# Another order of attention, a head loaded ahead, a head's parts per block, and the final norm inside the experts

## The chip, the cores and the metric

The kernel runs on one core of one Trainium2 chip. The metric is device time in microseconds (us), here of that core. TensorE (PE) does the matrix products, VectorE (DVE), ScalarE (ACT) and GpSimd (POOL) do elementwise work, SyncE (SP) issues most transfers. Each engine runs its instructions in order, and engines wait for one another through semaphores.

## What is computed

An encoder layer runs over two groups of tokens with shared weights: 1024 tokens ("prompt", the short group, g = 0) and 2048 tokens ("sample", the long group, g = 1), with D = 1024. The input is normalised, scaled and shifted by values made from a condition vector, and projected by w_in to latent queries and keys, a rotary key and four pooling groups u. Eight heads of attention (queries and keys 64 + 32 wide, values 64 wide) run within each group; beside them each pooling group takes mean minus value over a window of 2, 4, 8 or 16 tokens. Both go through an output projection to a gated residual. Then each of 16 experts takes its best tokens (128 of the short, 256 of the long group), runs them through a gated feed-forward of width 1024, and adds the weighted result to its tokens' rows. A last RMS normalisation with a gain closes it:

```python
def encoder_layer(x, c, ...):
    h = rmsnorm(x) * (1 + sc1) + sh1
    z = h @ w_in
    att = latent_attention(c_q, c_kv, k_pe, q_norm_g, kv_norm_g, w_uq, w_ukv)
    pool = multiscale_pool(u, w_pool, pool_scale)
    x = x + g1 * (jnp.concatenate([att, pool], axis=-1) @ w_out)
    h = rmsnorm(x) * (1 + sc2) + sh2
    return x + g2 * expert_choice_ffn(h, w_router, w_gate, w_up, w_down)
# trunk: return rmsnorm(encoder_layer(x, c), final_norm_g)
```

## The kernel before

Every product is made in three parts from a rounded high part and the remaining low part of each operand; so most data exists twice, ScalarE writes the high parts and VectorE or GpSimd the low ones. The program is a row of stages that hand results on through device memory (s_ct, s_qn, s_kn, s_v, s_x and so on). A stage ends for all engines at once: nothing of the next starts before its last store has landed. The order within a stage is written out by hand, per engine, and SyncE's queue of transfers is in order too. `build` (L2354) calls the stages.

`in_proj` (L100): w_ada and w_in come through a ring of five raw buffers, with SyncE waiting for the user of a buffer (`load_raw`, L211). The modulation values come from w_ada (`early`, `late`), the input blocks of 256 tokens are squared (`stats`, ScalarE), scaled by GpSimd (L279), transposed by TensorE (`turn`, L483; L493) and modulated by ScalarE (`modulate`, L300). `w_high` (L284, L287) and `w_low` (L401) split the w_in chunks. Then 24 tiles of 128 tokens are projected; per tile SyncE stores u (L253), s_ct and s_kr. After tile 17 SyncE also stores the four gate vectors, 4 bytes an element (L260 to L267), ahead of the load of a later input block (L209).

`latent_proj` (L597): six blocks of 512 tokens, for each 16 entries of ORDER (products for keys, queries, values and the rotary part), each followed by a high copy, a low subtraction and a store. Beside it GpSimd pools u in 12 jobs of 1024 columns (JOBS, L610): fetch by SyncE, 1 to 4 additions, a multiplication, a subtraction, and a store (L782) by SyncE at two points of each block.

`attention` (L935) is called for g = 1, then g = 0. It loads a head's queries, keys and values at its start (`load_qk`, L1037; `load_v`), memsets the rows with constants (L1310), and then takes heads in turn (HU = 2 or 4 heads have buffers), loading the next head in a loop while it works. For each block of 512 queries TensorE first makes a product for the row maxima (`unit`, L1106), then scores, exponentials, and values, and a sum. SyncE stores each block's result (L1047), folds the denominators and stores inverses (L1065). 

`experts` (L1940): for each expert, six chunks of weights (four of gate and up, two of down) are loaded, split by ScalarE (L2167) and VectorE (L2214) and multiplied. The down products (L2142 to L2144) run over 3 slots of 128 tokens for the first output half, then for the second; VectorE weighs each (L2269) into `ye`; after the last weighing GpSimd issues three indirect additions into s_x (L2078). Slot 0 holds the short group's tokens, slots 1 and 2 the long group's.

`final_norm` (L2280) is a stage of its own: 12 blocks of 256 tokens, through four buffers, loaded by SyncE (L2312), squared by ScalarE (L2330, L2333), scaled by VectorE (L2347, L2350) into a second set of buffers, and stored by ScalarE's queue.

## Time and profile before

| | us |
| --- | --- |
| median of 3 runs (lowest, highest) | 3949.04 (3944.26, 3949.94) |
| the profiled execution | 3950.72 |
| its span on the core | 3948.9 |
| TensorE busy in the span | 3577.4 (91%) |
| VectorE, ScalarE, GpSimd busy | 2024.3, 1885.9, 1348.1 |
| mean granted clock of TensorE (of full speed) | 0.941 |

Read it so: one execution was traced; the span runs from its first to its last instruction. Stages are seen by which lines run. In the trace the input projection takes 0 to 448, the latent projection to 656, the long group's attention to 1481, the short group's to 1717, output weights and output projection to 2090, selection to 2190, the experts to 3882, and the final normalisation to the end.

### The profile page before, as it was taken

To read this page: it belongs to the slowest core of one execution; us is meant where nothing else is said; L and a number is where in the kernel's file an instruction comes from. 1 tells how busy PE (TensorE), PEld (TensorE's weight loads), DVE (VectorE), ACT (ScalarE), POOL (GpSimd) and SP (SyncE) were. 2 spreads that over 40 slices of the span, in tenths; PEclk is the share of its full clock that TensorE was granted. 3 is DMA by queue.
4 is the path that set the end of the run, shared out by engine and by line. 5 is a ranking of instruction groups with operands and counts; after the bars stand their busy time and mean duration, and the time that the engine had idled before them with its cause. 6 is when DMAs were issued, how large, how long until landed. Compare 5 with 4: busy or idle time off the path is not lost. (4 is left out here: it accounts for less than half of the span.)

```text
span 3948.9 us, 54396 instructions
## 1 busy us (share of the span) xinstructions
PE 3577.4 (91%) x19090; PEld 3094.5 (78%) x19090; DVE 2024.3 (51%) x3145; ACT 1885.9 (48%) x3250; POOL 1348.1 (34%) x1008
## 2 busy tenths in 40 slices
PE   7999795999999998969993799999999999999991
PEld 5999684777777765747772799999999999999990
DVE  3332353888888876832226644444444444444433
ACT  3433221888888886843330334443443444444433
POOL 1111175988888887842221000000000000000000
PEclk8999897999999998989995899999999999999995
DMA  6444599022122206236541354455444444454437
GB/s 229 160 157 91 195 394 302 18 44 43 43 44 44 43 8 129 49 110 189 176 157 51 128 160 151 147 159 159 147 150 147 142 147 150 156 159 154 144 101 276
DMA packets 363781, 538.93 MB, mean 136 GB/s; under 512 B 38816, under 2 KB 256208, under 8 KB 360656
## 3 DMA queue, kind: packets, MB, share of 16 engines
q1 hardware_dynamic: 339600, 448.60, 36.4%
q0 software_dynamic: 13824, 50.34, 5.2%
q10 hardware_dynamic: 10176, 37.75, 2.4%
q8 instruction: 92, 1.51, 0.2%
q14 instruction: 89, 0.73, 0.1%
HBM read 394.07 MB, written 142.46 MB: 136 GB/s over the span
## 5 line engine op out<-in xcount | busy, mean ns | idle before, releaser
L1314 POOL TENSOR_TENSOR att_pr<-att_e,att_pr 128x512 fp32r<-128x512 f32 x640 | 812.6, 1292 | 152.1 <-ACT att_pr L1201 141.5
L2078 POOL DMA_INDIRECT s_x<-moe_ye,moe_to_add x48 | 90.9, 1893 | 1437.6 <-DVE moe_ye L2269 1427.8
L1245 DVE TENSOR_REDUCE att_mx<-att_m_ps 128x1 f32<-128x512 f32 x640 | 423.5, 682 | 116.0 <-PE att_m_ps L1106 106.2
L2214 DVE TENSOR_TENSOR keep_wl<-keep_raw,keep_wh 128x1024 fp32r<-128x1024 f32 x380 | 440.0, 1220 | 33.6 <-ACT keep_wh L2167 33.6
L2167 ACT ACTIVATE keep_wh<-keep_raw 128x1024 fp32r<-128x1024 f32 x380 | 369.9, 1045 | 126.0 <-PE moe_d_ps L2144 126.0
L1147 PE MATMUL att_o_ps<-att_pr,att_v 128*128 128x512 f32 x1280 | 410.3, 402 | 4.8 <-POOL att_pr L1314 4.6
L1195 ACT ACTIVATE att_e<-att_s_ps 128x512 f32<-128x512 f32 x640 | 378.4, 591 | 69.7 <-PE att_s_ps L1135 24.2
L1201 ACT ACTIVATE att_pr<-att_e 128x512 fp32r<-128x512 f32 x640 | 402.8, 629 | 18.4 <-issue 2.7
L1267 DVE TENSOR_TENSOR att_acc_ps<-att_acc_ps,att_e 128x512 f32<-128x512 f32 x544 | 375.0, 689 | 16.6 <-ACT att_e L1195 11.0
L2194 ACT ACTIVATE moe_silu<-moe_a_ps 128x384 f32<-128x384 f32 x128 | 62.9, 492 | 645.1 <-PE moe_u_ps L2117 645.1
L2115 PE MATMUL moe_a_ps<-moe_xh,keep_wh 128*128 128x384 f32 x1024 | 345.5, 337 | 2.1 <-DVE moe_xl L2222 2.1
L2252 DVE TENSOR_TENSOR moe_hf<-moe_u_ps,moe_silu 128x384 f32<-128x384 f32 x128 | 71.3, 557 | 536.5 <-ACT moe_silu L2194 536.5
L2117 PE MATMUL moe_a_ps<-moe_xh,keep_wl 128*128 128x384 f32 x1024 | 344.7, 337 | 0.0
L2116 PE MATMUL moe_a_ps<-moe_xl,keep_wh 128*128 128x384 f32 x1024 | 344.7, 337 | 0.0
L2117 PE MATMUL moe_u_ps<-moe_xh,keep_wl 128*128 128x384 f32 x1024 | 344.1, 336 | 0.0
L2115 PE MATMUL moe_u_ps<-moe_xh,keep_wh 128*128 128x384 f32 x1024 | 344.1, 336 | 0.0
L2116 PE MATMUL moe_u_ps<-moe_xl,keep_wh 128*128 128x384 f32 x1024 | 344.1, 336 | 0.0
L2142 PE MATMUL moe_d_ps<-keep_wh,moe_hh 128*128 128x512 f32 x768 | 312.0, 406 | 0.0
L2144 PE MATMUL moe_d_ps<-keep_wh,moe_hl 128*128 128x512 f32 x768 | 303.6, 395 | 0.0
L2143 PE MATMUL moe_d_ps<-keep_wl,moe_hh 128*128 128x512 f32 x768 | 302.7, 394 | 0.0
L1147 PEld LDWEIGHTS att_o_ps<-att_pr,att_v 128*128 128x128 f32 x1280 | 243.5, 192 | 67.6 <-POOL att_pr L1314 12.0
L1106 PE MATMUL att_m_ps<-att_k,att_q 96*128 96x512 f32 x640 | 236.8, 412 | 60.6 <-DMA att_k<-s_kr 60.6
(276 smaller groups left out, 7675.3 us busy)
## 6 DMA issues: line engine op xcount, KB each, us to landing
keep_raw<-w_gate SPq DMA_DIRECT2D x64, 1024.0 KB, 5.1
keep_raw<-w_up SPq DMA_DIRECT2D x64, 1024.0 KB, 7.6
keep_raw<-w_down SPq DMA_DIRECT2D x64, 1024.0 KB, 6.6
inp_raw<-w_ada SPq DMA_DIRECT2D x48, 512.0 KB, 5.9
s_ct<-inp_ct SPq DMA_DIRECT2D x24, 640.0 KB, 3.1
prj_ct<-s_ct SPq DMA_DIRECT2D x6, 2560.0 KB, 15.2
s_kn<-prj_out SPq DMA_DIRECT2D x24, 512.0 KB, 11.8
s_qn<-prj_out SPq DMA_DIRECT2D x24, 512.0 KB, 11.9
```

The lines of the kernel that those rows point to most:

```text
L1147: mm = nc.tensor.matmul(o_ps[b % 2][:, :], v[:, h, kt, :], pr[:, s % RING, a, :], start=(kt == 0 and a == 0), stop=(kt == NT - 1 and a == 1))
L1195: nc.scalar.activation(e[:, s % RING, :], s_ps[s % 2][:, :], ACT.Exp, scale=SCALE).then_inc(exp_done, 1)
L1201: nc.scalar.activation(pr[:, s % RING, 0, :], e[:, s % RING, :], ACT.Copy).then_inc(hi_done, 1)
L1245: nc.vector.tensor_reduce(mx[:, u % CB, u // CB:u // CB + 1], m_ps[u % MB][:, :], AX, ALU.max).then_inc(max_part, 1)
L1267: step = nc.vector.tensor_tensor(acc_ps[:, :], acc_ps[:, :], e[:, s % RING, :], ALU.add)
L1314: nc.gpsimd.tensor_tensor(pr[:, s % RING, 1, :], e[:, s % RING, :], pr[:, s % RING, 0, :].bitcast(F32), ALU.subtract).then_inc(lo_done, 1)
L2115: nc.tensor.matmul(out, hi, xh[:, k, :], start=(k == 0), stop=False)
L2116: nc.tensor.matmul(out, hi, xl[:, k, :], start=False, stop=False)
L2117: mm = nc.tensor.matmul(out, lo, xh[:, k, :], start=False, stop=(k == KD - 1))
L2142: nc.tensor.matmul(out, h_hi, wh[:, c % 2, k, :], start=(k == 0), stop=False)
L2167: nc.scalar.activation(wh[:, s, part, :], raw[:, s, part, :], ACT.Copy).then_inc(w_hi_done, 1)
L2214: nc.vector.tensor_tensor(wl[:, s, part, :], raw[:, s, part, :], wh[:, s, part, :].bitcast(F32), ALU.subtract).then_inc(w_lo_done, 1)
```

## The change

- The input projection: ScalarE makes the first three high parts of w_in before the first modulations and one after; VectorE's low parts follow them; in tile 0 the transposes of block 1 come after the u products, and ScalarE's statistics of tile 0 come ahead of the next modulation. The gates are stored by ScalarE's queue after tile 17.
- The latent projection: pooling in 24 jobs of 512 columns, four a block at entries 2, 6, 10 and 14 of ORDER; GpSimd's last addition writes the sum to diff, and VectorE makes the difference from the mean in one operation (`difference`). The first two fetches of u are issued before w_uq. Rows of ones and zeros are stored to s_rows. After block 2's stores SyncE loads the short group's first head (queries, keys, rows: 7 parts) into kept memory.
- Attention: the short group comes first; head 0's values are loaded at its start and heads 1 to 3 by `load_part`, eight parts a head, rows of constants among them (in place of GpSimd's memsets). During its 16 blocks SyncE loads one part a block of the long group's two first heads, and waits for all of them before the last store.
- Experts: the last expert's down products go slot by slot, both halves of one slot after another, and each slot's addition is issued once its two weighings are done. The final normalisation is part of this stage: in place, in four buffers that lie in the raw weights' memory; the first four blocks (the short group's) are loaded after slot 0's addition, the others after those of slots 1 and 2. VectorE takes block j - 2 behind weighing j. The final_norm stage is gone.

The diff, cut to its core:

```diff
-                if n == len(LATE) + 1:
-                    sp.wait_ge(mod_done, len(EARLY) + len(LATE))
-                    for a, part in enumerate((2, 5)):
-                        for g in range(2):
-                            at = (2 * a + g) * D
-                            sp.dma_start(w["s_gates"][0, at:at + D].rearrange("(k p) -> p k", p=P),
-                                         keep["modc"][:, g, part * KD:(part + 1) * KD],
-                                         allow_slow_non_contiguous=True).then_inc(gates_stored, 16)
...
+            def store_gates():
+                act.wait_ge(mod_done, len(EARLY) + len(LATE))
+                for a, part in enumerate((2, 5)):
+                    for g in range(2):
+                        at = (2 * a + g) * D
+                        act.dma_start(w["s_gates"][0, at:at + D].rearrange("(k p) -> p k", p=P),
+                                      keep["modc"][:, g, part * KD:(part + 1) * KD],
+                                      allow_slow_non_contiguous=True).then_inc(gates_stored, 16)
...
             for half in range(2):
-                if half:
-                    for k in range(PAIRS):
-                        w_high(k)
+                for k in range(3 * half, PAIRS if half else 3):
+                    w_high(k)
                 for c in (2 * half, 2 * half + 1):
                     modulate(0, c)
...
+                    n = TB * b + j
+                    if n == 0:
+                        latent_stats(n)
                     if b + 1 < NB:
                         modulate(b + 1, 2 * j)
-                    latent_stats(TB * b + j)
+                    if n:
+                        latent_stats(n)
                     if b + 1 < NB:
                         modulate(b + 1, 2 * j + 1)
                     latent_high(TB * b + j)
+                    if TB * b + j == len(LATE) + 1:
+                        store_gates()
...
+            for k in range(2):
+                w_low(k)
+            copy_rows(2, u_ps[0][:, :])
+            w_low(2)
             for c in range(2):
                 h_low(0, c)
-            for i in range(2):
-                for k in (2 * i, 2 * i + 1):
-                    w_low(k)
-                copy_rows(2 + i, u_ps[i][:, :])
+            w_low(3)
+            copy_rows(3, u_ps[1][:, :])
...
+                    if n == 0:
+                        for c in range(2):
+                            h_low(1, c)
...
-                    if n == 0:
-                        turn(1, 0)
-                    if b + 1 < NB:
+                    if b + 1 < NB and n:
                         turn(b + 1, 2 * j + 1)
...
+                    if n == 0:
+                        for c in range(2):
+                            turn(1, c)
...
+def load_part(sp, w, g, n, heads, i, part, sem):
+
+    S = SEQS[g]
+    NT = S // P
+    tokens = slice(STARTS[g], STARTS[g] + S)
+    q, k, v = heads[i]
+    if part < 4:
+        dst, src = ((q[0:NOPE], w["s_qn"][:, n + i, :, tokens]), (q[NOPE:QK], w["s_qr"][:, n + i, :, tokens]),
+                    (k[0:NOPE], w["s_kn"][:, n + i, :, tokens]), (k[NOPE:QK], w["s_kr"][:, :, tokens]))[part]
+        src = src.rearrange("l r t -> r l t")
+    elif part < 7:
+        dst, row = ((k[QK:QK + 1, 0], 1), (k[QK:QK + 1, 1], 0), (q[QK:QK + 1, 1], 0))[part - 4]
+        src = w["s_rows"][row:row + 1, 0:S]
+    else:
+        dst = v
+        src = w["s_v"][TILE0[g]:TILE0[g] + NT, :, (n + i) * 2 * VD:(n + i + 1) * 2 * VD].rearrange("t p c -> p t c")
+    sp.dma_start(dst.bitcast(F32), src).then_inc(sem, 16)
+
+
 def latent_proj(nc, w, keep):
...
-    SPAN = min(SEQS)
+    SPAN = BANK
...
+    JOBS_PER = len(JOBS) // NB
+    POINTS = [PER * (i + 1) // JOBS_PER - 2 for i in range(JOBS_PER)]
...
+                for lev in range(c + 1):
+                    r = 1 << lev >> 1
+                    lo, hi = 2 * r + (lev == 0), SPAN + 2 * PAD - 2 * r + (lev > 0)
+                    src = sums[:, (lev - 1) % 2] if lev else x
+                    before, behind = (src[:, lo - r:hi - r], src[:, lo + r:hi + r]) if lev else (src[:, lo - 1:hi - 1], src[:, lo:hi])
+                    if lev == c:
+                        cut = slice(PAD - lo, PAD - lo + SPAN)
+                        nc.gpsimd.tensor_tensor(diff[:, n % 2], before[:, cut], behind[:, cut], ALU.add).then_inc(total_ready, 1)
+                    else:
+                        done = step(nc.gpsimd.tensor_tensor(sums[:, lev % 2, lo:hi], before, behind, ALU.add))
+                        pool.wait_ge(summed, done)
...
             load(0)
+            for n in range(2):
+                fetch(n)
             sp.dma_start(qraw[:], w["w_uq"][0].rearrange("(k p) n -> p k n", p=P)).then_inc(q_in, 16)
...
-                    if at in (PER // 3, 2 * PER // 3):
-                        n = 2 * b + int(at > PER // 2)
+                    if at in POINTS:
+                        n = JOBS_PER * b + POINTS.index(at)
...
+                if b == SEQS[0] // BANK:
+                    sp.wait_ge(w_lo_done, ALL_PIECES)
+                    for slot in range(SLOTS):
+                        sp.wait_ge(stored[slot], 16 * b)
+                    for part in range(HEAD_LOADS - 1):
+                        load_part(sp, w, 0, 0, head_tiles(keep, 0, None), 0, part, ahead_in)
...
+            sp.wait_ge(ahead_in, 16 * (HEAD_LOADS - 1))
...
+                c = JOBS[n][1]
+                first, last = ends_of(n)
+                a, b = PAD * first, SPAN - PAD * last
+                dve.wait_ge(total_ready, n + 1)
+                nc.vector.scalar_tensor_tensor(diff[:, n % 2, a:b], diff[:, n % 2, a:b], 1.0 / WINDOWS[c],
+                                               u[:, n % 2, PAD + a:PAD + b], ALU.mult, ALU.subtract).then_inc(diff_ready, 1)
...
+                    if n in POINTS:
+                        difference(JOBS_PER * b + POINTS.index(n))
...
-            load_qk(0, 0)
-            for i in range(HU):
-                sp.dma_start(k[NOPE:QK, i].bitcast(F32), w["s_kr"][:, :, tokens]
-                             .rearrange("l r t -> r l t")).then_inc(kpe_in, 16)
-            load_v(0, 0)
-            for i in range(1, HU):
-                load_qk(i, i)
-                load_v(i, i)
+            if g == 0:
+                load_v(0, 0)
+            for i in range(READY, HU):
+                for part in range(HEAD_LOADS):
+                    load_part(sp, w, g, 0, heads, i, part, rest_in[i])
...
+                    if g == 0:
+                        n = it * NG + b
+                        load_part(sp, w, 1, 0, head_tiles(keep, 1, None), n // HEAD_LOADS, n % HEAD_LOADS, ahead_in)
...
             over_heads(sp, body)
+            if g == 0:
+                sp.wait_ge(ahead_in, 2 * 16 * HEAD_LOADS)
             store(ITERS, -1)
             fold(ITERS, -1)
             store_inverses(ITERS, -1)
...
-            for row, value in ((k[QK:QK + 1, :, 0, :], 1.0), (k[QK:QK + 1, :, 1, :], 0.0), (q[QK:QK + 1, :, 1, :], 0.0)):
-                nc.gpsimd.memset(row.bitcast(F32), value).then_inc(rows_set, 1)
...
+        fin = raw[:].rearrange("p s k n -> p (s k n)").rearrange("p (r j d) -> p r j d", r=R, j=2)
+        gain = rows[:, 0, :]
...
+        def down(last, j):
+
+            return (j // 2, j % 2) if last else (j % SLOTS, j // SLOTS)
...
             over_experts(sp, body)
+            sp.wait_ge(turned, E * KD)
+            sp.dma_start(gain, w["final_norm_g"].partition_broadcast(P)).then_inc(gain_in, 16)
+            sp.wait_ge(w_lo_done, (E * CHUNKS - 1) * PIECES)
+            for b in range(BLOCKS):
+                if b == 0:
+                    sp.wait_ge(added[0], 16 * E)
+                if b == EARLY_BLOCKS:
+                    for s in range(1, SLOTS):
+                        sp.wait_ge(added[s], 16 * E)
+                if b >= R:
+                    sp.wait_ge(y_stored[b % R], 16 * (b // R))
+                src = w["s_x"][b * 2 * P:(b + 1) * 2 * P, :].rearrange("(j p) d -> p j d", p=P)
+                sp.dma_start(fin[:, b % R], src).then_inc(fin_in[b % R], 16)
 
...
-                pool.wait_ge(ye_done, (e + 1) * DOWNS)
+                if not last:
+                    pool.wait_ge(ye_done, (e + 1) * DOWNS)
...
+                    if last:
+                        pool.wait_ge(ye_done, e * DOWNS + 2 * (s + 1))
...
+                for j in range(DOWNS):
+                    s, n = down(last, j)
                     c = GU + n
-                    pe.wait_ge(w_lo_done, (e * CHUNKS + c) * PIECES)
-                    for s in range(SLOTS):
...
+            for b in range(BLOCKS):
+                act.wait_ge(fin_in[b % R], 16 * (b // R + 1))
+                for j in range(2):
+                    if 2 * b + j >= 2:
+                        act.wait_ge(squared, 2 * b + j - 1)
+                    nc.scalar.activation(rows[:, 1 + j, :], fin[:, b % R, j, :], ACT.Square, scale=float(D) ** -0.5,
+                                         accum_out=ms[:, 2 * b + j:2 * b + j + 1]).then_inc(squared, 1)
+                act.wait_ge(squared, 2 * b + 2)
+                nc.scalar.activation(ms[:, 2 * b:2 * b + 2], ms[:, 2 * b:2 * b + 2], ACT.Sqrt,
+                                     bias=eps[:, 0:1]).then_inc(std_done, 1)
+                if b >= 1:
+                    store(b - 1)
+            store(BLOCKS - 1)
...
+                            weigh(e, last, j)
+                if last:
+                    for j in range(DOWNS):
+                        weigh(e, last, j)
+                        if j >= 2:
...
+            def normalise(b):
+
+                if b == 0:
+                    dve.wait_ge(gain_in, 16)
+                dve.wait_ge(std_done, b + 1)
+                nc.vector.reciprocal(ms[:, 2 * b:2 * b + 2], ms[:, 2 * b:2 * b + 2]).then_inc(rstd_done, 1)
+                dve.wait_ge(rstd_done, b + 1)
+                for j in range(2):
+                    nc.vector.scalar_tensor_tensor(fin[:, b % R, j, :], fin[:, b % R, j, :], ms[:, 2 * b + j:2 * b + j + 1],
+                                                   gain, ALU.mult, ALU.mult).then_inc(y_done, 1)
...
-        latent_proj(nc, w, keep)
-        for g in (1, 0):
-            attention(nc, w, keep, g)
+        with ExitStack() as ahead:
+            tile(ahead, "ahead0", [P, 4 * SEQS[0]], F32R, side="right")
+            latent_proj(nc, w, keep)
+            tile(ahead, "ahead1", [P, 2 * (4 * SEQS[1] + SEQS[1] // P * 2 * VD)], F32R, side="right")
+            for g in range(2):
+                attention(nc, w, keep, g)
...
-        moe_ctx.close()
-        final_norm(nc, w, keep)
```

## Rows read from the trace of the kernel before

**Rows 1.** Page, part 2: TensorE busy tenths in 40 slices of 98.7 us
```profile
PE   7999795999999998969993799999999999999991
```

**Rows 2.** Timeline (start us, duration, engine, line, operation, [idle before]) from 0; a window
```profile
21.15 8.83 SPq L232 DMA_DIRECT2D inp_raw<-w_ada  x2
...
26.98 2.25 ACT L287 ACTIVATE inp_wh<-inp_raw 128x1184 fp32r<-128x1184 f32 x2
...
23.33 0.17 DVE L381 TENSOR_TENSOR keep_modc<-inp_c_ps,inp_biasc 128x8 f32<-128x8 f32 x1 [0.65 <-PE inp_c_ps L530]
...
63.93 1.97 PE L493 MATMUL inp_t_ps<-keep_ident,inp_x 128*128 128x128 f32 x8 [5.09 <-POOL inp_x L279]
...
65.00:70.00 5.00, 5.00 (x28) 5.00 (x27) 2.81 (x9) 4.31 (x11) 0.00 (x0) 0.55 0.00 0
```

**Rows 3.** Timeline of SyncE's queue and of ScalarE, 345 to 401 us
```profile
348.08 0.36 SPq L253 DMA_DIRECT2D s_ut<-inp_ut  x1
350.89 2.92 SPq L265 DMA_DIRECT2D s_gates<-keep_modc  x4
353.86 2.05 SPq L209 DMA_DIRECT2D inp_x<-x_sample  x1
362.71 0.36 SPq L253 DMA_DIRECT2D s_ut<-inp_ut  x1
383.66 0.36 SPq L253 DMA_DIRECT2D s_ut<-inp_ut  x1
400.42 0.36 SPq L253 DMA_DIRECT2D s_ut<-inp_ut  x1
...
375.49 1.06 ACT L294 ACTIVATE inp_junk<-inp_x 128x1024 f32<-128x1024 f32 x1 [11.95 <-DMA inp_x<-x_sample]
```

**Rows 4.** Latent projection: a window (DMA share, GB/s last), timelines, a line, a landing
```profile
455.00:640.00 185.00, 168.17 (x720) 137.73 (x720) 98.88 (x136) 56.04 (x100) 125.81 (x95) 0.94 1.02 388
...
645.87 0.34 SPq L782 DMA_DIRECT2D s_diff<-prj_diff  x1
655.99 0.73 SPq L1037 DMA_DIRECT2D att_q<-s_qn  x1
...
677.10 9.52 PE L1106 MATMUL att_m_ps<-att_k,att_q 96*128 96x512 f32 x16 [41.36 <-DMA att_k<-s_kr]
...
L723 POOL TENSOR_TENSOR prj_sums<-prj_u 128x1039 f32<-128x1039 f32 x12 | 23.0, 1917 | 60.4 <-DMA prj_u<-s_ut 60.2 <-POOL prj_diff L751 0.2
...
prj_u<-s_ut SPq DMA_DIRECT2D x8, 516.0 KB, 12.2
```

**Rows 5.** Between the two groups' attentions, the second's end; a landing
```profile
1495.35 4.74 PE L1106 MATMUL att_m_ps<-att_k,att_q 96*128 96x512 f32 x8 [19.27 <-DMA att_k<-s_kr]
...
1481.56 0.64 SPq L1037 DMA_DIRECT2D att_q<-s_qn  x1
...
1709.51 0.34 SPq L1065 DMA_DIRECT2D s_rden<-att_rden  x1
1711.19 0.48 SPq L1047 DMA_DIRECT2D s_att<-att_att  x1
...
att_v<-s_v SPq DMA_DIRECT2D x4, 512.0 KB, 9.7
```

**Rows 6.** The last expert and the final normalisation: timelines, window, landing
```profile
3836.07 0.74 DVE L2269 SCALAR_TENSOR_TENSOR moe_ye<-moe_d_ps,keep_gate,moe_g 128x512 f32<-128x512 f32 x1
3862.50 0.75 DVE L2269 SCALAR_TENSOR_TENSOR moe_ye<-moe_d_ps,keep_gate,moe_g 128x512 f32<-128x512 f32 x1 [4.84 <-PE moe_d_ps L2144]
3892.98 2.48 DVE L2350 SCALAR_TENSOR_TENSOR fin_y<-fin_x,fin_ms,fin_gain 128x1024 f32<-128x1024 f32 x2
...
3881.98 43.08 SPq L2312 DMA_DIRECT2D fin_x<-s_x  x12
...
3905.00:3945.00 40.00, 0.00 (x0) 0.00 (x0) 21.17 (x24) 19.01 (x40) 0.00 (x0) 0.50 1.03 421
...
s_x<-moe_ye,moe_to_add POOLq DMA_INDIRECT x3, 6.8
```

More of the change, by code:

```diff
@@ L715, in set_pads @@
                     pads(nc.gpsimd.memset(u[:, n % 2, PAD + SPAN:], 0.0))
+            for i in range(2):
+                nc.gpsimd.memset(rows[:, i, :].bitcast(F32), float(i)).then_inc(rows_set, 1)
             for n in range(2):
@@ new lines, in _ @@
+                if first or last:
+                    pool.wait_ge(total_ready, n + 1)
+                for here, at, e0 in ((first, 0, 0), (last, SPAN - PAD, PAD)):
+                    if here:
+                        done = step(nc.gpsimd.tensor_tensor(ends[:, e0:e0 + PAD], diff[:, n % 2, at:at + PAD],
+                                                            edge[:, c, e0:e0 + PAD], ALU.mult))
+                        pool.wait_ge(summed, done)
+                        done = step(nc.gpsimd.tensor_tensor(diff[:, n % 2, at:at + PAD], ends[:, e0:e0 + PAD],
+                                                            x[:, PAD + at:2 * PAD + at], ALU.subtract))
+                        pool.wait_ge(summed, done)
@@ L790, in _ @@
             sp.dma_start(edge[:].rearrange("p a b -> p (a b)"), w["k_edge"].partition_broadcast(P)).then_inc(edge_in, 16)
[L791 to L792 removed]
             load(1)
+            sp.wait_ge(rows_set, 2)
+            sp.dma_start(w["s_rows"].rearrange("l (p c) -> p l c", p=P), rows[:].bitcast(F32)).then_inc(rows_stored, 16)
             for b in range(NB):
@@ L2354, in build @@
+            for b in range(DOWNS - 2, BLOCKS):
+                normalise(b)
 def build(nc, w):
```

252 lines of the change are left out of this document (108 added, 144 removed).

## The prediction

> **What bounds the kernel now.** I read the page's strip of busy tenths first. TensorE is at 9 tenths or more nearly everywhere in the experts (slices 22 to 39) and drops at a few seams: the first slice, slices 7 and 16 to 18, the last two [rows 1]. So TensorE's work sets the time, and a change that leaves its products alone, as this one does, can only win or lose at seams. For each seam I took the timeline: what TensorE waits for, and what SyncE (which issues most loads and stores, in order) stood at. The reader should see five holes. (1) At the head TensorE waits 5.09 us for GpSimd's normalised input at 63.93, and the clock granted in 65 to 70 is 0.55, half of full speed [rows 2]. (2) A 1 MB input load stands behind four scattered gate stores, and ScalarE waits 11.95 us for it [rows 3]. (3) TensorE idles 41.36 us between projection and attention [rows 4]. (4) It idles 19.27 us between the two attentions [rows 5]. (5) From the last product to the end, 67 us belong to the final normalisation: first load issued at 3881.98, span 3948.9 [rows 6].
>
> The sum is made against the profiled execution, 3950.7 us (span 3948.9), which is 1.7 above the median shown, 3949.0.
>
> **A, head of the input projection: -13.** SyncE's load of w_ada stands from 21.15 to 29.98, since its buffer is freed by the low split of the first w_in chunk. ScalarE copies that chunk's high part only at 26.98, behind two modulations [rows 2]. With the copies ahead, the low split can follow the bias add of 23.33 (0.17): at some 24.9 with one 1.1 us copy. That starts the weight chain 5.1 us earlier. The transposes of block 1, moved behind the u products, no longer make TensorE wait: 5.1 again (GpSimd, 5.09 late, has the u products' time). Cold clock: work from 63.93 to about 69.5 runs at 0.55 and would take half, so 2.8 [rows 2]. Sum 13.0. Bounds: 8 (no clock gain, 3 of the first term) and 13. The modulations on ScalarE come 3.4 us later (three copies), which their wait for the transposes hides.
>
> **B, gate stores: -8.4.** The x load issued at 353.86 lands at 375.49, 21.6 us for 1 MB, and the stores of s_ut, one per tile, are 14.63 us apart before it (348.08, 362.71), then 20.95 (383.66) and 16.76 (400.42) [rows 3]. The excess, 6.3 + 2.1, is the price of the gates. After the change SyncE goes from its stores to the x load at once, while ScalarE issues the gates in its own queue at about the same time (its high parts of that tile are done, and it waits for products there, so four issues, 2.92 us on SyncE [rows 3], delay nothing). x is needed only at about 363.5, 10 us or more after its issue, where a fetch of half its size takes 12.2 with DMA saturated [rows 4] and DMA has room here. So I take both excesses away. Bounds: 0 and 8.4. What the rows of before do not show is whether x waited because it stood behind the gates in one queue, or because their 4-byte elements hold the engines themselves. The Trainium skill ("DMA: Bandwidth & Descriptors") has a rule for either: by its section "Issuing engines are not separate DMA queues", DMAs of any issuing engine share the same 16 engines, and another issuer saves only the time to issue, by which B would be about 0. By its section "Queues, rings and completion order", each engine takes turns between queues packet by packet, by which x passes between the gates' packets and B would stand. No run here shows either yet; the first is a rival below.
>
> **C, projection to attention: -20.** In 455 to 640 DMA is saturated: share 1.02, 388 GB/s, and TensorE's 720 products take 168.17 us, 7.0 per 30 [rows 4]. The page's pooling holds SyncE to 645.87 (the last difference store), after which six stores wait to be issued; the stage ends at 655.99, when the first attention load goes, and TensorE starts at 677.10 [rows 4]. After: pooling no longer holds those stores, but the head's 1.5 MB is added. At 388 GB/s 3.1 + 1.5 MB take 12 us from 640, so the end is some 652 to 656; I take 655.5, about today's. Then the first attention unit starts 0.5 later, at 656.0 instead of 677.1: -21.1. Against this +1.3 at the stage's start, since u's first two fetches (0.5 MB at 388 GB/s) are put ahead of w_uq. The constant rows (0, 1) are memsets beside the start, and their waits on SyncE are short. Bounds: the stage ends at 649.8 (655.99 less its last 10.1, plus 3.9 for 1.5 MB) or 659.9, stage entry 0.5 or 4.1 (1495.35 - 1481.56 less the 9.7 of a landing [rows 5]), start 0 or 3: gain 10 to 27.
>
> The pooling is now 24 jobs of half length, four per block. Two buffers alternate, so fetch, adds, difference and SyncE's turn must fit in two jobs, 14.0 us. A fetch of 516 KB lands in 12.2 [rows 4], half of it in 6.1 to 12.2; the adds, half of 1.917 us each, one to four a job, are 2.4 on average; the difference, now on VectorE, is 0.75 (its 128x512 operation in [rows 6]). So 9.3 to 15.4 against 14.0. I take no loss; the upper end is a rival. VectorE's 24 differences (18 us in all) lie beside TensorE: it is busy 98.88 of 185 us [rows 4]. Behind each wait for GpSimd's sum on VectorE stand the low splits, which SyncE's stores and TensorE's banks wait for.
>
> **D, between the attentions: -8.** 1481.56 to 1495.35 is a head load, 13.8 us, that leaves the seam; 0.5 remains, so -13.3. Added: SyncE waits for the last of the 16 parts (1 MB of v) before the short group's last store. It is issued after the previous block's inverses, 1709.51, and lands in 2.7 (388 GB/s) to 9.7 (rows of 0.5 MB); I take 7, so SyncE is free at 1716.5 instead of 1711.19, +5.3 [rows 5]. Behind that wait stand the last attention store, fold and inverses, and the stage ends with them. Gain 5 to 12. Two 1 MB v parts and 14 parts of q and k in 16 blocks are hidden: a block takes about 14 us and a part 3 to 10.
>
> **E, the end: -24.4.** The prompt's slot is now produced first. Its second product waits for the low split of chunk 5 (VectorE is at it until 3836.07) instead of 3834.5, +1.5, so its add is issued at about 3842.6 and lands 6.8 later, 3850 [rows 6]. The four prompt blocks then take as long as today's first one, 3881.98 to 3892.98 plus 2.48: 13.5, so 3863.5 for the first normalisation, which VectorE runs between weighings. This holds the fourth weighing until 3864.2; the sixth product (4.84 + 0.75 apart) ends at 3869.8, its weighing at 3870.6 behind a normalisation, and the last add lands at 3878. Eight sample blocks then take 8 x 5.0 (2.1 MB in and out at 421 GB/s [rows 6]) plus 7 for the last block's path: 3925. That is -24. The stage's own end, beginning and constant loads save 0.4. Bounds: 18 where a buffer (now normalised in place, so load + normalise + store before it is reused) cycles in over 20 us and costs a block or the delayed weighings cost more, 30 where the weighings are not delayed. I let the low end reach 15 for both.
>
> Costed at nothing: attention's inner steps, which are as before; the GpSimd memsets of rows that go, which lay beside the head loads of the seams.
>
> Sum: 13.0 + 8.4 + 20 + 8 + 24.4 = 73.8, so 3876.9 for an execution like the profiled one, 3875 against the median. 0.2%, 8 us, is about what a measurement of this kernel can tell from no change.
>
> **The rivals.**
> R1, the gates still delay x: their 4-byte elements hold the engines whatever queue they are in, so x, issued among them, lands after 21.6 us as before. For: that landing [rows 3]. Against: x has a queue without them, and 10 us of slack. B = 0: 3883.
>
> R2, pooling is late: the half-size fetch still lands in 12.2, so 15.4 against 14.0, 12 pairs, 16 us lost [rows 4]. For: DMA share 1.02. Against: half the bytes. C = 4: 3891.
>
> R3, slower than before: in the same loop a fetch lands in 21.6, as the load of [rows 3] behind scattered stores did. A pair of jobs takes 21.6 + 2.4 + 0.75 = 24.8, 10.8 over 14.0, and 12 pairs 129 us, against 74 gained: about 4004. Its place is SyncE in the latent projection, where stores, head parts and loads queue behind the difference's wait. It decides the sign once the loop exceeds 14.0 + 74/12 = 20.2 us, a landing of 17. Against: a full queue shrinks when the loop is slow.
>
> R4, the end: normalisations ahead of weighings in VectorE's order, or in-place buffers, leave E at 15: 3884.
>
> R5, the change doesn't do what it says: the head or long group's parts are still in flight at the seams, so C and D fall away: 3903.
>
> **How the numbers follow.** The forecast 0.58, R1 0.08, R2 0.14, R4 0.08, R5 0.05: all faster by over 0.2%. R3 0.05 is slower, and a loop near 20 us (within 0.2%) 0.02. All gains at their low ends give 3911, all at their high ones 3858. The range goes from all gains at their high ends to past R2 with one more term short, and takes in R1, R2 and R4; R5 and R3, 1 in 10 together, are left out: 3858 to 3900.
>
> **What would show it.** Attention's first unit directly behind the stage's end, with about 20 idle before it, not 41; 6 to 10 at the second seam, not 19; s_ut stores 14.6 apart at 362 to 400; TensorE's gap at the first transposes gone; the first load of the final blocks before the last weighing, and 45 to 50 us from the last add's landing to the end. I am wrong if the projection's pace slows (TensorE waiting for VectorE behind a GpSimd sum), if the gates' stretch keeps its two long steps, or if the last load parts hold the seams.

## The result and the profile after

The changed kernel takes 3902.82 us (median of 4 runs, 3894.14 to 3905.21) where the kernel before takes 3947.28 in the runs beside it: a ratio of 0.9884, 95% interval 0.9866 to 0.9901. It is faster by some 45 us, not by the 74 of the forecast, and 2.8 us outside the range. The sum below is made between the two profiled executions (spans 3948.9 and 3901.7, 47.2 apart).

| stretch | before | after | measured | forecast |
| --- | --- | --- | --- | --- |
| A: start to the store of u of tile 17 | 348.08 | 334.94 | -13.1 | -13.0 |
| B: from there to the third store after it | 52.3 | 53.1 | +0.7 | -8.4 |
| from there to the latent projection's first product | 60.3 | 60.6 | +0.3 | 0 |
| C: that product to attention's first unit | 216.4 | 199.1 | -17.3 | -20 |
| short group's attention, without the idle time behind it | 217.0 | 228.8 | +11.9 | 0 |
| long group's attention, likewise | 799.0 | 798.3 | -0.6 | 0 |
| D: idle time between the two, and behind the second | 19.3 + 8.5 | 10.1 + 9.6 | -8.2 | -8 |
| output weights to the experts' first transposes | 472.4 | 469.4 | -3.0 | 0 |
| E: from there to the end | 1755.6 | 1737.8 | -17.9 | -24.4 |

A, C and D came within 3 us. B gave nothing, the short group's attention lost 12 us that no term had, and E gave three quarters. The stretch to the experts took 469 to 474 us in the runs below with nothing changed in it, so its 3.0 is scatter.

The page's busy tenths of TensorE after, against [rows 1]. The seventh slice, in which TensorE waited for the first attention, goes from 5 tenths to 8; the seam between the attentions has moved from the sixteenth to the tenth slice with the order; the last slice is at 3 instead of 1.

```profile
PE   7999798998999999969983899999999999999993
```

The head, from the timeline after (SyncE, VectorE, TensorE, then a window with the granted clock third from its end, then SyncE), against [rows 2]:

```profile
19.70 3.73 SPq L232 DMA_DIRECT2D inp_raw<-w_ada  x2
...
21.66 1.38 DVE L409 TENSOR_TENSOR inp_wl<-inp_raw,inp_wh 128x1184 fp32r<-128x1184 f32 x1
...
58.82 1.04 PE L504 MATMUL inp_t_ps<-keep_ident,inp_x 128*128 128x128 f32 x8
...
65.00:70.00 5.00, 5.00 (x48) 4.17 (x46) 1.16 (x5) 3.70 (x12) 3.80 (x2) 1.00 0.88 298
...
334.94 0.36 SPq L253 DMA_DIRECT2D s_ut<-inp_ut  x1
```

The load of w_ada stands for 3.7 us instead of 8.8, because the first low split runs at 21.66, ahead of the modulations; the transposes of block 1 run in one go of 1.04 us (1.97 before) with no wait, and the granted clock from 65 to 70 is 1.00 where it was 0.55; tile 17's u is stored 13.1 us earlier.

The gates, from ScalarE's queue, SyncE's, ScalarE itself, the list of DMAs (KB each, us to landing) and, for 344 to 350 us, the two queues (q1 is SyncE's, q10 ScalarE's; packets, MB, share of the engines' time), against [rows 3]:

```profile
334.88 0.46 ACTq L329 DMA_DIRECT2D s_gates<-keep_modc  x1
...
337.76 1.45 SPq L209 DMA_DIRECT2D inp_x<-x_sample  x1
...
349.66 0.36 SPq L253 DMA_DIRECT2D s_ut<-inp_ut  x1
...
371.13 0.36 SPq L253 DMA_DIRECT2D s_ut<-inp_ut  x1
...
388.02 0.36 SPq L253 DMA_DIRECT2D s_ut<-inp_ut  x1
...
362.96 1.06 ACT L286 ACTIVATE inp_junk<-inp_x 128x1024 f32<-128x1024 f32 x1 [11.62 <-DMA inp_x<-x_sample]
...
inp_x<-x_sample SPq DMA_DIRECT2D x1, 1024.0 KB, 25.2
...
s_ct<-inp_ct SPq DMA_DIRECT2D x1, 640.0 KB, 20.1
...
q1 hardware_dynamic: 50, 0.26, 100.0%
q10 hardware_dynamic: 51, 0.00, 9.6%
```

The four gate stores go out from ScalarE's queue from 334.88 to 337.7, the load of x at 337.76 from SyncE's, a queue without gates. It lands after 25.2 us, where the one of before took 21.6, and ScalarE again waits for it, 11.62 us. Ahead of it in SyncE's queue stands tile 17's store of s_ct, issued at 336.91 among the gates: it lands after 20.1 us (3.1 before, when the gates came behind it), and x 5.9 us later. The last two lines show that the two queues take turns, 50 packets against 51; but in that time SyncE's queue moved only 0.26 MB. The two long steps between stores of u are still there, 21.5 and 16.9 us.

The latent projection, from four timelines, against [rows 4]:

```profile
559.55 0.38 SPq L831 DMA_DIRECT2D prj_u<-s_ut  x1
...
574.07 1.06 POOL L795 TENSOR_TENSOR prj_sums<-prj_u 128x527 f32<-128x527 f32 x1 [14.03 <-DMA prj_u<-s_ut]
...
580.13 0.79 PE L922 MATMUL prj_ps<-prj_wv,prj_ct 128*128 128x512 f32 x1 [7.84 <-DVE prj_out L1010]
...
647.72 0.39 SPq L1125 DMA_DIRECT2D att_v<-s_v  x1
...
647.75 2.94 PE L1191 MATMUL att_m_ps<-keep_ahead 96*128 96x512 f32 x5 [13.45 <-PEq L671]
```

A fetch of u issued at 559.55, behind the head's 1.5 MB, reaches GpSimd 14 us later; VectorE stands at that difference in order and TensorE waits 7.84 us for its low split. TensorE's last product ends 185.7 us after its first (175.0 before). The stage ends with the first attention transfer at 647.72, and the first unit follows at once (41.36 us of idle time are now 13.45).

The short group's attention, and the seam behind it:

```profile
773.70 0.85 SPq L644 DMA_DIRECT2D keep_ahead<-s_v  x1
...
774.60 2.42 SPq L1120 DMA_DIRECT2D att_q<-s_qn  x1
...
781.07 0.77 SPq L1141 DMA_DIRECT2D att_rden<-att_den  x1
...
790.03 0.18 DVE L1371 RECIPROCAL att_rden<-att_rden 128x4 f32<-128x4 f32 x1 [4.39 <-DMA att_rden<-att_den]
...
874.62 0.43 SPq L644 DMA_DIRECT2D keep_ahead<-s_v  x1
...
881.78 0.49 SPq L1130 DMA_DIRECT2D s_att<-att_att  x1
...
886.65 9.52 PE L1191 MATMUL att_m_ps<-keep_ahead 96*128 96x512 f32 x16 [10.07 <-PEq L1032]
```

Here a 1 MB part of the long group, then a head of the short group (1.8 MB), then the 2 KB of denominators are issued, in this order in SyncE's queue. VectorE takes them up 9 us after their issue, where the median landing of these transfers in this stretch is 2.1, and VectorE waits 4.39 us for them before its reciprocal. At 874.62 the last part goes, and the last attention store waits for it to 881.78, 7.2 us (forecast: 7).

The end, against [rows 6]:

```profile
3840.94 2.54 POOL L2200 DMA_INDIRECT s_x<-moe_ye,moe_to_add  x1 [5.65 <-DVE moe_ye L2421]
...
3853.66 1.06 ACT L2340 ACTIVATE moe_rows<-keep_raw 128x1024 f32<-128x1024 f32 x1 [15.56 <-DMA keep_raw<-s_x]
...
3868.01 1.06 ACT L2340 ACTIVATE moe_rows<-keep_raw 128x1024 f32<-128x1024 f32 x1 [6.10 <-DMA keep_raw<-s_x]
```

The last addition is issued at 3840.94 and the first sample block is squared at 3853.66. Three blocks later, at the fourth sample block, ScalarE waits 6.10 us for a load, to 3868.01. Before, 81.1 us lay between the last addition's issue and the end; now 60.8 do, where the forecast's steps gave 54.

### The profile page after: what moved, and what is told of

It reads as the page before. It is cut to its first block and busy times, and to the rows that moved or that the text cites. A ratio compares the mean times of both kernels' runs of the same rounds, so it can differ in the third digit from the quotient of the medians.

```text
span 3901.7 us, 54523 instructions
## 1 busy us (share of the span) xinstructions
PE 3570.0 (92%) x19090; PEld 3087.0 (79%) x19090; DVE 2027.1 (52%) x3169; ACT 1882.6 (48%) x3250; POOL 1279.2 (33%) x1010
## 5 line engine op out<-in xcount | busy, mean ns | idle before, releaser
L1232 PE MATMUL att_o_ps<-att_pr,keep_ahead 128*128 128x512 f32 x1024 | 327.3, 401 | 2.5 <-POOL att_pr L1401 2.5
L1232 PEld LDWEIGHTS att_o_ps<-att_pr,keep_ahead 128*128 128x128 f32 x1024 | 194.9, 192 | 50.1 <-POOL att_pr L1401 6.1
L1216 PE MATMUL att_s_ps<-keep_ahead 97*128 97x512 f32 x544 | 224.1, 412 | 5.2 <-issue 3.7
```

Source lines behind the costliest of these rows:

```text
L1232: mm = nc.tensor.matmul(o_ps[b % 2][:, :], v[h][:, kt, :], pr[:, s % RING, a, :], start=(kt == 0 and a == 0), stop=(kt == NT - 1 and a == 1))
```

## The experiments

All are edits of the changed kernel, one run each, but for the three edits together, with five. Durations of one run scatter: the input projection by 3 us either way, the stretch to the experts by 2.5; so each edit is read in its own stretch. The stage durations are TensorE's and SyncE's as in the table.

### The gates: one tile group later, and in longer pieces

```diff
-                    if TB * b + j == len(LATE) + 1:
+                    if TB * b + j == len(LATE) + 4:
                         store_gates()
```

> The changed kernel with one edit: ScalarE stores the four gate vectors after tile 20 of the input projection, where no input block is left to load, instead of after tile 17. Against the profile of the changed kernel, where the input block issued at 337.8 lands after 25.2 us, ScalarE waits 11.6 us for it, two steps between the stores of u are 21.5 and 16.9 us, and the latent projection's first product runs at 448.6. Theory (the 4-byte elements hold the DMA engines, whichever queue they are in): the block lands in under 12 us, both steps are 14.7, the first product of the latent projection runs near 440 and the whole is 8 to 9 us shorter. Rival (the block is late for its own reasons: one queue, 1 MB among the stores of tiles): landing and steps stay, 0 us. Second rival (the gates' time comes back at the stage's end, which waits for them): the steps are 14.7 but the first product stays within 3 us of 448.6.

```diff
-                        act.dma_start(w["s_gates"][0, at:at + D].rearrange("(k p) -> p k", p=P),
+                        act.dma_start(w["s_gates"][0, at:at + D].rearrange("(p k) -> p k", p=P),
```

> The changed kernel with the gates stored at the same place, by the same queue, with the same bytes, but 32 bytes of each partition in one run (128 runs a vector instead of 1024 elements of 4 bytes); the gate vectors' order is thereby another one, and all else is as it was. Theory (the number of elements is the price): as with the late store, steps of 14.7 us, 8 to 9 us gained at the latent projection's first product. Rival (a store from ScalarE's queue beside the load shares the engines by turns, whatever its pieces): the steps stay 21 and 17 us, 0 us.

Of the first: two stores of u in SyncE's queue (tiles 19 and 20), the latent projection's first product, and the landing of x:

```profile
365.95 0.36 SPq L253 DMA_DIRECT2D s_ut<-inp_ut  x1
...
380.59 0.36 SPq L253 DMA_DIRECT2D s_ut<-inp_ut  x1
...
440.99 0.80 PE L922 MATMUL prj_ps<-prj_ct,prj_wk 128*128 128x512 f32 x1 [18.34 <-DMA prj_ct<-s_ct]
...
inp_x<-x_sample SPq DMA_DIRECT2D x1, 1024.0 KB, 5.5
```

Of the second: the product, and the landings of x and of the gates:

```profile
440.77 0.80 PE L922 MATMUL prj_ps<-prj_ct,prj_wk 128*128 128x512 f32 x1 [18.37 <-DMA prj_ct<-s_ct]
...
inp_x<-x_sample SPq DMA_DIRECT2D x1, 1024.0 KB, 5.4
...
s_gates<-keep_modc ACTq DMA_DIRECT2D x4, 4.0 KB, 1.9
```

The steps are 14.6 us, x lands in 5.5, and the projection begins 7.6 us earlier than in the changed kernel; in the second, with the same bytes at the same moment from the same queue but in 128 pieces a vector, x lands in 5.4 and the projection begins 7.8 earlier. (The second puts the gates down in another order, so what it computes is not the layer; only its time is read.) From tile 17's store to the third after it both take 43.9 us, 9.2 less than the changed kernel, and 8.4 less than the kernel before. So the price is the number of pieces, 4096 of 4 bytes: ScalarE's own queue for them did not lower it, and fewer pieces did. In the first the store of s_ct issued among the late gates (at 382.56) lands after 19.3 us, as the one of the changed kernel did, but no load stands behind it. Nothing came back at the stage's end. Whether x would have passed the gates with no store ahead of it, no run shows. The first of the two rules of the Trainium skill that the prediction weighed ("DMA: Bandwidth & Descriptors", "Issuing engines are not separate DMA queues": one set of 16 engines whoever issues) agrees with the traces, with 25.2 us from another queue against 21.6. The second rule of the Trainium skill (the same page, "Queues, rings and completion order": an engine takes turns between queues packet by packet) agrees as well, with the 50 and 51 packets above; what failed is the step from it to "x passes". SyncE's packets had their turns and were slow all the same, 50 of them filling the engines' time for 6 us.

### The parts: odd blocks, then even blocks

```diff
-                        load_part(sp, w, 1, 0, head_tiles(keep, 1, None), n // HEAD_LOADS, n % HEAD_LOADS, ahead_in)
+                        load_part(sp, w, 1, 0, head_tiles(keep, 1, None), *AHEAD[n], ahead_in)
```

In the first, AHEAD has the 1 MB parts in blocks 1, 3, 5, 7, 9, 11; in the second in 2, 4, 6, 8, 9, 10.

> The changed kernel with the 16 parts of the long group's two heads in another order over the 16 blocks of the short group's attention: the 1 MB parts in blocks in which no head of the short group is loaded, the 8 KB rows and smaller parts in the others, the last two rows. Theory (a block's 2 KB transfer of denominators waits behind 1 MB parts in SyncE's queue, VectorE waits for it in order, 14.0 us in all in the changed kernel against 2.5 in the kernel before; that is why the short group's attention takes 228.6 us and not 216.5): VectorE's waits before the reciprocals fall to some 6 us and the stretch from the first product of the short group's attention to the long group's first unit falls from 238.9 to about 231. Rival (the attention is slower by its start, when heads 1 to 3 are loaded, or by the order of its heads): the stretch stays within 2 us of 238.9.

SyncE's queue and VectorE in the first:

```profile
752.52 0.44 SPq L645 DMA_DIRECT2D keep_ahead<-s_v  x1
...
759.90 0.53 SPq L1142 DMA_DIRECT2D att_rden<-att_den  x1
...
768.93 0.18 DVE L1372 RECIPROCAL att_rden<-att_rden 128x4 f32<-128x4 f32 x1 [4.45 <-DMA att_rden<-att_den]
```

It went the wrong way: waits of 5.55, 5.61, 4.45 and 5.29 us, the short group's attention 236.4 us instead of 228.8 (242.2 to the long group's first unit, where 231 was expected), the whole 8 us longer. My edit had put every large part straight ahead of a head's load and the denominators behind both. The rival is refuted all the same: the same bytes in another order moved the stretch by 8 us. The lead to the second came from these rows.

> The changed kernel with the long group's 16 parts in another order again. In the first reordering I had the parity wrong: a part issued in an odd block is followed at once, in SyncE's queue, by the next head's load of the short group (1.8 MB) and then by the 2 KB transfer of denominators; its four 1 MB parts in odd blocks gave waits of 5.55, 5.61, 4.45 and 5.29 us. Here 1 MB parts go into blocks 2, 4, 6 and, where no head is loaded any more, 8, 9 and 10; rows into the odd blocks before that and the last. Theory (what counts is how many bytes stand in the queue just ahead of the denominators): VectorE's waits before reciprocals fall from 14.0 us (changed kernel) to 2.5 to 4, as in the kernel before, and the stretch from the short group's first product to the long group's first unit from 238.9 to about 229, or to 224 where the last part, now 8 KB, lets SyncE pass to the last store at once (its wait is 7.2 us in the changed kernel). Rival (any megabyte more in this stage costs its share): waits and stretch within 3 us of the changed kernel's.

SyncE, VectorE and TensorE in the second:

```profile
750.95 0.53 SPq L1142 DMA_DIRECT2D att_rden<-att_den  x1
...
756.94 0.42 SPq L645 DMA_DIRECT2D keep_ahead<-s_v  x1
...
756.25 0.18 DVE L1372 RECIPROCAL att_rden<-att_rden 128x4 f32<-128x4 f32 x1 [0.70 <-DMA att_rden<-att_den]
...
873.94 6.53 PE L1192 MATMUL att_m_ps<-keep_ahead 96*128 96x512 f32 x11 [5.58 <-PEq L1033]
```

Waits are 0.45, 0.45, 0.70 and 0.11 us, the attention takes 216.0 us (217.0 before the change; 221.6 to the long group's first unit, where 224 to 229 was expected), and the first long unit comes after 5.58 us of idle time instead of 10.07, as the last part is a row of 8 KB. The two orders, with equal bytes, differ by 20 us in the attention. Its span is 3889.9 us (3901.7) although its input projection was 4.8 us slower than the changed kernel's.

### The latent projection: spread, doubled, undone

```diff
+                        part = n - 3 * JOBS_PER
+                        if 0 <= part < HEAD_LOADS - 1:
+                            load_part(sp, w, 0, 0, head_tiles(keep, 0, None), 0, part, ahead_in)
...
-                    for part in range(HEAD_LOADS - 1):
-                        load_part(sp, w, 0, 0, head_tiles(keep, 0, None), 0, part, ahead_in)
```

> The changed kernel with the seven parts of the short group's first head issued one at each pooling point of blocks 3 and 4 of the latent projection instead of all after block 2. In the changed kernel a fetch of u behind them lands after 14 us, VectorE waits 14.3 us for the pooling and TensorE 7.8 us at 580. Theory 1 (the stage's length is set by its DMA bytes at 388 GB/s: 195.3 us from its first product to the first attention transfer before, 199.1 with 1.5 MB more, which is 3.9 us at that rate): TensorE's wait at 580 goes, its last product comes 8 us earlier, and the stage still ends 199 us after its first product; 0 us for the whole. Theory 2 (the wait at 580 is the loss): the stage ends 8 to 10 us earlier.

TensorE in it:

```profile
575.64 0.50 PE L923 MATMUL prj_ps<-prj_wv,prj_ct 128*128 128x512 f32 x1 [2.60 <-DVE prj_out L1011]
...
608.78 0.79 PE L923 MATMUL prj_ps<-prj_wv,prj_ct 128*128 128x512 f32 x1 [3.37 <-DVE prj_out L1011]
...
647.81 4.73 PE L1192 MATMUL att_m_ps<-keep_ahead 96*128 96x512 f32 x8 [12.40 <-PEq L671]
```

The wait of 7.84 became two of 2.60 and 3.37; the stage from first product to first unit took 198.1 us against 199.1. That bears out theory 1 in its length, not in its detail: the last product came no earlier against the first (185.7 us both times), where 8 us earlier was expected. The waits fell by only 1.9 us, and the products took 1.9 us more (TensorE busy 172.1 us in the stage against 170.2): after the second wait they ran slowly again, with a granted clock of 0.81 from 608 to 624, where the changed kernel has 1.00 in 599 to 624.

> The kernel of head_spread (parts of the first head one at each pooling point) with the first five parts loaded a second time, into the same place, at the following points: 1.5 MB more. Theory (bytes over 388 GB/s set the latent projection's length, which was 195.3 us in the kernel before, 199.1 in the changed one, and 198.1 with the parts spread): 3.9 us more, 202, with TensorE's products ending when they did or up to 4 us later. Rival (the length is set by TensorE and its waits, the bytes fit beside them): 198, 0 us.

First product and first unit:

```profile
449.38 0.80 PE L927 MATMUL prj_ps<-prj_ct,prj_wk 128*128 128x512 f32 x1 [18.52 <-DMA prj_ct<-s_ct]
...
653.36 4.73 PE L1196 MATMUL att_m_ps<-keep_ahead 96*128 96x512 f32 x8 [17.91 <-PEq L671]
```

204.0 us: 5.9 more for 1.5 MB more, where 3.9 was expected and 0 by the rival. The last product stayed where it was (186.1 us after the first). Bytes set the stage's length here, at a somewhat higher price than their rate gives.

> The changed kernel with the short group's first head loaded at the start of its attention, by the same seven transfers, and not in the latent projection. Theory (the head's 1.5 MB cost the DMA-bound projection 3.9 us and save the seam a head's load): the stage from its first product to the first transfer of the attention falls from 199 to 195, TensorE's wait of 7.8 us at 580 goes, and the first unit comes 10 to 14 us after the stage's end, so that it stands 6 to 10 us later than in the changed kernel in all. Rival (the wait at 580 is what the load cost, 8 us, so that loading ahead gives nothing): first unit within 2 us of the changed kernel's 199.1 us after the first product.

First product, first transfer of the attention (SyncE), first unit:

```profile
450.79 0.80 PE L919 MATMUL prj_ps<-prj_ct,prj_wk 128*128 128x512 f32 x1 [18.29 <-DMA prj_ct<-s_ct]
...
645.55 0.73 SPq L644 DMA_DIRECT2D keep_ahead<-s_qn  x1
...
656.98 4.76 PE L1190 MATMUL att_m_ps<-keep_ahead 96*128 96x512 f32 x8 [26.48 <-DMA keep_ahead<-s_rows]
```

The stage to its end falls to 194.8 us, as expected; TensorE's wait does not go, as was expected too, but falls to two of 3.2 us in all. And the first unit follows 11.4 later, 206.2 us after the first product instead of 199.1. But the short group's attention then takes 223.9 us instead of 228.8 (VectorE's wait of 5.41 in its first block is gone, the second block's is 2.68 instead of 1.74), so that loading the head ahead was worth only 2 us net in this kernel, and the span is 3902.1, as against 3901.7.

From the first product to the last landing the DMA engines moved 373 to 376 GB/s in the kernel before, in the changed one and in these three alike, so the lengths follow the bytes. The kernel with no hold by pooling and no head (194.8) is as long as the one before with the hold (195.3).

### The end: room for the sample blocks

```diff
-                if b >= R:
-                    sp.wait_ge(y_stored[b % R], 16 * (b // R))
...
-                sp.dma_start(fin[:, b % R], src).then_inc(fin_in[b % R], 16)
+                dst = out[:, b] if b < R else late[b // R - 1][:, b % R].bitcast(F32)
+                sp.dma_start(dst, src).then_inc(fin_in[b], 16)
```

> The changed kernel with room in the final normalisation: the eight sample blocks are loaded into the memory of the split weights (high and low parts, free by then) without waiting for a store, and the normalised blocks are written into the four buffers of the raw weights. In the changed kernel ScalarE gets the first sample block at 3853.7 and the span ends at 3901.7, 48.0 later, with the DMA below 360 GB/s in many slices; in the kernel before, eight blocks took 8 x 5.0 us at 421 GB/s. Theory (normalising in place in four buffers ties each load to the store four blocks earlier, and that is the 6.5 us which the end falls short): from the first sample block to the end 40 to 43 us, 5 to 7 less. Rival (the end is set by bytes or by ScalarE's queue issuing stores between squares): 47 to 48, 0 us.

GpSimd and ScalarE at its end:

```profile
3847.34 2.54 POOL L2200 DMA_INDIRECT s_x<-moe_ye,moe_to_add  x1 [5.66 <-DVE moe_ye L2421]
...
3859.59 1.06 ACT L2340 ACTIVATE moe_rows<-keep_wh 128x1024 f32<-128x1024 f32 x1 [15.10 <-DMA keep_wh<-s_x]
```

From the first sample block's square to the end (span 3901.0) 41.4 us instead of 48.0, and 53.7 instead of 60.8 from the last addition's issue. The forecast's 54 was that of buffers that are not reused. ScalarE waits nowhere longer than 2.6 us between the sample blocks. This run began 2.5 us later at the projection and was 6.1 us later at the experts' first transposes by scatter, which is why its span isn't lower.

### The head of the input projection

The old order of its instructions was put back, first all of it, then only that of tile 0's transposes (`turn`), statistics and low parts of h.

> The changed kernel with the order at the head of the input projection put back (high parts of w_in behind the first modulations, VectorE's low parts behind both first h parts, the transposes of block 1 and the statistics of tile 0 where they were); the gates stay on ScalarE's queue. Theory (the head's order alone gives what the input projection gained, 12.1 us at the latent projection's first product, since the gates gave nothing): first product near 460.7, 10 to 12 us later than in the changed kernel's looks (448.6 to 453.4), and GpSimd's wait of 5 us before the transposes back. Rival (the stage's length scatters and the order gave about 5, which is what the first transposes of block 1 gained, 63.9 to 58.8): 455.

TensorE's transposes of block 1, and the store of tile 17:

```profile
63.51 1.97 PE L496 MATMUL inp_t_ps<-keep_ident,inp_x 128*128 128x128 f32 x8 [5.08 <-POOL inp_x L271]
...
347.14 0.36 SPq L253 DMA_DIRECT2D s_ut<-inp_ut  x1
```

> The changed kernel with only the second half of that put back: transposes of block 1 between the products of tile 0, its statistics and h parts as before; the high and low parts of w_in stay early. By the forecast's terms the early weights are worth 5.1 us and the moved transposes 5.1 and the cold clock 2.8: a first product 5 to 8 us later than in the changed kernel, 455 to 459 by its looks. Rival (the transposes' wait was covered, the early weights give it all): within 2 us of the changed kernel's 448.6 to 453.4.

```profile
60.80 1.97 PE L497 MATMUL inp_t_ps<-keep_ident,inp_x 128*128 128x128 f32 x8 [5.08 <-POOL inp_x L271]
...
344.46 0.36 SPq L253 DMA_DIRECT2D s_ut<-inp_ut  x1
```

Ten traces of kernels with the changed order (the changed kernel, the eight edits above and the three edits together, below) store tile 17's u between 332.3 and 338.3, 335.7 on average. Put back as a whole it is 347.1, 11.4 later, with the wait of 5.08 us back; the latent projection's first product is at 462.9 (expected 460.7; the rival's 455 is out). The moved transposes alone are worth 8.7 (forecast 7.9 with the cold clock; first product at 458.9), and with them back the granted clock from 60 to 65 is 0.50, where the changed kernel has 1.00. The early weights are worth 2.7 (forecast 5.1). Both are single runs, against a scatter of 3 us.

### Three edits together

Gates after tile 20, parts as in the even order, room at the end.

> Three edits together: gates stored after tile 20, the order of the parts as in parts_even, room in the final normalisation. If the three causes are independent, against the changed kernel 8 + 10 to 15 + 5 to 7 us less, 23 to 30: a median near 3876 where the changed kernel has 3902.8, a ratio of about 0.982 to the kernel before. Rival (they overlap, or one was only moved): less than 15 us in all, 3888 or more.

Five runs: 3875.65 us (3866.8 to 3878.63) against 3944.73 before, ratio 0.9828 (0.9814 to 0.9841). The interval lies clear of the changed kernel's. The three causes add up: 27 us below its median, where 23 to 30 were expected. Its profiled run, the fastest of the five (span 3864.8), has 200.1 us for the projection, 215.1 for the short group's attention and 54.0 from the last addition to the end.

## Why the prediction was wrong, step by step

The range ended at 3900, and 3902.82 is 2.8 above it; the prediction's own sum of low ends, 3911, was not passed. The reading of the strip at its start left out three drops, at slices 5, 22 and 23 (7, 3 and 7 tenths; the last two are the selection before the experts); no term of the sum hangs on them.

**A** was right in sum: 13.0 forecast, 13.1 measured, 11.4 by undoing it. Of its terms the transposes (with the clock) were right and the early weights half as large as thought: SyncE's next two loads of w_ada stand 3.3 and 4.5 us, where they stood 0.9 and 2.5 before. That the sum came out to 0.1 us is in part luck.

**B** is the first step that failed: "x passes" on its own queue. The bound of 0 and rival R1 (0.08) were what happened. I took the place behind the gates in one queue to be the price; the late and the coarse store show that it is the number of elements. SyncE's own queue was not free either: x stood in it behind the store of s_ct, which the gates held for 20.1 us, and x landed 5.9 us after that. x's slack of 10 us was there, and the gates took more.

**C**: the mechanism was right and the size of one term off. The stage ended where the old one did plus the head's bytes (195.3 us from its first product, then 199.1: 3.8 more, and 1.5 MB at 388 GB/s is 3.9). I had put the end at today's, since the six stores were no longer held; but DMA, not the hold, set it. The term was put at +0.8 (1.3 for the fetches less 0.5) and measured 3.8. In R2 pooling was late, and it was, by one fetch of 14 us, not by each. TensorE's pace did slow, the sign named: its last product ended 10.7 us later against the first than before. But the stage's end then came 13.4 us behind it instead of 20.3, as the bytes set it, and so the unit came after 13.45 us of idle time and not some 20. R3 did not occur.

**The short group's attention** is the failure that no term had: "Two 1 MB v parts and 14 parts of q and k in 16 blocks are hidden". The parts themselves are. What they delay, the 2 KB transfer behind them in the same queue for which VectorE waits in order, isn't. Over the first fourteen of its sixteen blocks VectorE's waits before reciprocals grew from 2.5 to 14.0 us, the attention by 11.9, and without the collision it takes 216.0 again. I asked whether the parts would be in time and not what is queued behind them.

**D** held: 8.2 for 8, with the last part's wait of 7.2 us as taken.

**E**: the steps to the last addition were right (the last weighing was put to end 35 us after the first began, at 3836.07; the last addition is issued 34.2 after it, 3806.73 to 3840.94), and the sample blocks' term was wrong: 47 us is the time of eight blocks with free buffers; in place, each load waits for the store four blocks earlier. That was rival R4, taken at 0.08 with 15 for E (measured: 17.9). With room the end took the forecast's 54 us.

With B at 0, 12 us lost in attention and 7 at the end the forecast's sum is 46, and 44 with C's shortfall. The direction was right; the range left out that three terms fall short together.

## What to carry to other kernels

Where a queue carries both large prefetches and a small transfer on which an in-order engine waits, place the large ones behind the small one's landing: the same bytes in two orders differed by 20 us. A prefetch into a stage whose DMA is saturated was paid here at about the DMA's rate, whatever wait it seemed to cause. Scattered 4-byte elements cost the same from either of the two queues tried, so move them to where nothing that is waited for is due, or make their pieces longer.

## What was not expected of the hardware

Four stores of 4 KB, 4096 pieces in all, delayed the landing of a 640 KB store on the other queue from 3.1 to 20.1 us and of a 1 MB load behind it from 5.5 to 25.2, though the two queues took turns; the same 16 KB in 512 pieces landed in 1.9 us (median) and did not. And TensorE's wait of 7.84 us in the projection, made into two of 2.60 and 3.37, left the last product where it was: the granted clock was 0.93 from 575 to 600 and 0.81 from 608 to 624 (0.80 and 1.00 in the changed kernel), and the time saved in waits was spent in slower products.
